# VectorE's small steps read one operand from PSUM: layer-norm variance, modulation columns and two norms' scaling in a two-block transformer kernel on one core

## What is computed

```python
# first block, layers 0 and 1
mod_x = split((silu(c) @ ada_w[layer] + ada_b[layer])[:, None, :], 6)      # and mod_c from c_ctx
h_x = modulate(rmsnorm(x, norm_g[layer, 0]), mod_x[0], mod_x[1])           # h * (1 + scale) + shift
o_x, o_c = mixer_ab(...) or mixer_c(...)                                   # attention
x = x + mod_x[2] * o_x
h_x = modulate(rmsnorm(x, norm_g[layer, 1]), mod_x[3], mod_x[4])
x = x + mod_x[5] * swiglu(h_x, ...)
# second block, 4 layers, each with three of
x = layer_norm(ALPHA * x + y, ln_g[i, j], ln_b[i, j])
# layer_norm: mu = mean(x); var = mean((x - mu)**2); (x - mu) * rsqrt(var + 1e-5) * g + b
```

## Time and profile before

| | |
|---|---|
| median of 3 runs | 2805.81 us (2800.55 to 2807.04) |
| profiled execution: span from first to last instruction | 2794.0 us |
| profiled execution: its time with what lies around the span | not listed apart; the median is 11.8 us above the span |
| TensorE matmul busy | 2636.5 us (94%) |
| GpSimd busy | 1819.7 us (65%) |
| ScalarE busy | 1467.7 us (53%) |
| VectorE busy | 1126.3 us (40%) |
| HBM | 150 GB/s |
| mean granted TensorE clock | 0.963 |

### The profile page before, as it was taken

The page is one execution under the profiler, slowest core; times in us unless marked ns, Lnnn a source line. Parts: engine busy times, 40 slices in busy tenths (PEclk is TensorE's granted clock), DMA queues, the critical chain, the costliest instruction groups (busy, mean ns, idle before and its releaser), DMA issues.

```text
span 2794.0 us, 52649 instructions
## 1 busy us (share of the span) xinstructions
PE 2636.5 (94%) x19840; PEld 2501.8 (90%) x19840; DVE 1126.3 (40%) x2642; ACT 1467.7 (53%) x2586; POOL 1819.7 (65%) x770
## 2 busy tenths in 40 slices
PE   7998889999999999989999998999999999989998
PEld 5897779999997799988899988899978999988998
DVE  5227634122155521135443365433443433553334
ACT  5336734445445554444555576555645555555655
POOL 0446647878875778863578865488645688535886
PEclk7999999999999999999999999999999999989998
DMA  6324424555553555542345543355423455323554
GB/s 228 125 102 153 146 95 166 180 178 184 183 167 126 180 168 183 179 142 81 121 151 181 185 138 128 107 189 180 157 92 121 144 181 183 127 76 121 173 180 136
DMA packets 115637, 421.75 MB, mean 151 GB/s; under 512 B 12832, under 2 KB 14112, under 8 KB 114976
## 3 DMA queue, kind: packets, MB, share of 16 engines
q1 hardware_dynamic: 115200, 417.00, 45.2%
q10 hardware_dynamic: 288, 2.62, 0.2%
HBM read 418.52 MB, written 1.05 MB: 150 GB/s over the span
## 4 chain that ended last, share of the span: by engine, by line
PE 58%; issue 18%; POOL 15%; DVE 5%; ACT 2%; DMA 1%; POOLq 0%; SPq 0%; DVEq 0%; ACTq 0%
POOL ring_low L2444 15%; PE bank L610 10%; PE bank L611 10%; PE bank L616 10%; PE bank L601 7%; PE bank L602 7%; PE bank L603 7%; PE bank L916 2%; PE bank L885 2%; PE bank L766 1%; DMA ring<-in_units 1%; PE bank L705 1%; PE bank L934 1%; PE bank L706 1%; PE bank L899 1%
## 5 line engine op out<-in xcount | busy, mean ns | idle before, releaser
L2444 POOL TENSOR_TENSOR ring_low<-ring,ring_high 128x1024 fp32r<-128x1024 f32 x766 | 1819.5, 2405 | 954.5 <-ACT ring_high L1243 744.0
L610 PE MATMUL bank<-high,ring_high 128*128 128x256 f32 (+1 forms) x3372 | 857.1, 290 | 3.2 <-ACT ring_high L1243 1.8
L611 PE MATMUL bank<-low,ring_high 128*128 128x256 f32 (+1 forms) x3372 | 849.5, 288 | 0.0
L610 PEld LDWEIGHTS bank<-high,ring_high 128*128 128x128 f32 x3372 | 647.0, 192 | 10.5 <-ACT ring_high L1243 3.5
L611 PEld LDWEIGHTS bank<-low,ring_high 128*128 128x128 f32 x3372 | 647.2, 192 | 6.5
L1475 ACT ACTIVATE ring_high<-ring 128x1024 fp32r<-128x1024 f32 x448 | 468.3, 1054 | 90.8 <-DMA ring<-in_units 90.8
L616 PE MATMUL bank<-high,ring_low 128*128 128x256 f32 (+1 forms) x3372 | 491.3, 288 | 0.3 <-POOL ring_low L2444 0.3
L616 PEld LDWEIGHTS bank<-high,ring_low 128*128 128x128 f32 x3372 | 444.9, 192 | 6.1 <-POOL ring_low L2444 0.5
L1243 ACT ACTIVATE ring_high<-ring 128x1024 fp32r<-128x1024 f32 x337 | 351.4, 1054 | 101.1 <-DMA ring<-in_units 99.7
L601 PE MATMUL bank<-hid_high,ring_high 128*128 128x256 f32 x1232 | 349.5, 284 | 9.8 <-DVE hid_low L2091 7.4
L602 PE MATMUL bank<-hid_low,ring_high 128*128 128x256 f32 x1232 | 348.6, 283 | 0.0
(11 more groups left out here) (226 smaller groups left out, 3468.3 us busy)
## 6 DMA issues: line engine op xcount, KB each, us to landing
ring<-in_units SPq DMA_DIRECT2D x785, 512.0 KB, 3.4
xt<-in_x SPq DMA_DIRECT2D x2, 1024.0 KB, 8.4
nbias<-in_bias ACTq DMA_DIRECT2D x1, 1536.0 KB, 7.2
vt<-in_mem ACTq DMA_DIRECT2D x1, 1024.0 KB, 7.1
out_x<-xt SPq DMA_DIRECT2D x8, 128.0 KB, 1.7
consts<-in_consts SPq DMA_DIRECT2D x1, 832.0 KB, 9.9
cols<-in_cols SPq DMA_DIRECT2D x1, 639.0 KB, 6.3
consts<-in_consts SPq DMA_DIRECT2D x1, 512.0 KB, 7.5
```

Of the source, the lines that this page charges most:

```text
L610: first = pe.matmul(out, w[0], x[0], start=start, stop=False)
L611: pe.matmul(out, w[0], x[1], start=False, stop=False)
L2444: pool.tensor_tensor(whole(ring_low, u), whole(ring, u), whole(ring_high, u).bitcast(fp32), ALU.subtract).then_inc(unit_ready, 1)
```

## The change

1. **Modulation columns.** ACT's copy `ada_cols_out` is gone, 24 instructions, and with it ACT's two waits and the SBUF tensor `ada_cols`. DVE waits for PE's transposes itself. Its first step becomes a `tensor_reduce` from 16 columns of the bank to 8 columns of the same bank, its second reads these from PSUM and the bias from SBUF. The bank is free for PE's next group when this second step is done.
2. In both attentions `modulations` moves from the end of DVE's step to just behind the copies of the first head's transposed probabilities, ahead of the next item's row minima.
3. **Layer norm.** L1794 and L1795 write into columns 2 and 3 of bank 6, and L1796 reads them from there.
4. **Norms f00 and f10.** The reciprocal goes to columns 0 to 255 of bank 7, and `scaled` reads it from there. Norms f01, n10 and n11 keep `rstd`.

```diff
-                def ada_cols_out(l, g, b=7):
-                    act.wait_ge(*when("ada_cols", l, g))
-                    if (l, g) != (0, 0):
-
-                        act.wait_ge(*when("mods", *((l, g - 1) if g else (l - 1, 11))))
-                    act.activation(ada_cols[:, :], banks[b][:, 0:16], ACT.Copy
-                                   ).then_inc(*mark(act_done, "ada_colsread", l, g))
...
-                def norm(st, dim, eps, b=7, between=None):
+                def norm(st, dim, eps, b=7, inverse=None):
...
-                    link(dve.reciprocal(rstd[:, 0:T], rstd[:, 0:T]))
+                    link(dve.reciprocal(rstd[:, 0:T] if inverse is None else inverse, rstd[:, 0:T]))
...
                     dve.tensor_copy(var[:, 0:4], b[:, 0:4]).then_inc(*mark(dve_done, st, "mean"))
-                    ledger.at[(st, "statsread")] = ledger.at[(st, "mean")]
                     dve.wait_ge(*when(st, "mean"))
-                    dve.tensor_scalar(var[:, 2:3], var[:, 0:1], var[:, 0:1], var[:, 2:3], ALU.mult, ALU.subtract)
-                    link(dve.tensor_scalar(var[:, 3:4], var[:, 1:2], var[:, 1:2], var[:, 3:4], ALU.mult, ALU.subtract))
-                    dve.tensor_scalar(var[:, 2:4], var[:, 2:4], 0.0, EPS_LN, ALU.min, ALU.subtract
+                    dve.tensor_scalar(b[:, 2:3], var[:, 0:1], var[:, 0:1], var[:, 2:3], ALU.mult, ALU.subtract)
+                    link(dve.tensor_scalar(b[:, 3:4], var[:, 1:2], var[:, 1:2], var[:, 3:4], ALU.mult, ALU.subtract))
+                    dve.tensor_scalar(var[:, 2:4], b[:, 2:4], 0.0, EPS_LN, ALU.min, ALU.subtract
                                       ).then_inc(*mark(dve_done, st, "var"))
+                    ledger.at[(st, "statsread")] = ledger.at[(st, "var")]
...
-                def scaled(st, l, which, s, part, at=0, tiles=range(KD)):
+                def scaled(st, l, which, s, part, rows=rstd[:, 0:T], tiles=range(KD)):
...
                             dve.scalar_tensor_tensor(out=tmp(k), in0=X(k, s), scalar=gain(l, which, s, k),
-                                                     in1=rstd[:, at:at + T], op0=ALU.mult, op1=ALU.mult
+                                                     in1=rows, op0=ALU.mult, op1=ALU.mult
...
                         out_pt(s, 0)
+                        if ada_fill(ada, 5 * s):
+                            modulations(*ada_fill(ada, 5 * s)[0])
                         if shallow:
                             lowest(s + 1, 0)
...
-                        if ada_fill(ada, 5 * s):
-                            modulations(*ada_fill(ada, 5 * s)[0])
...
-                def modulations(l, g):
+                def modulations(l, g, b=7):
 
-                    dve.wait_ge(*when("ada_colsread", l, g))
-                    parts = ada_cols[:, :].rearrange("p (m e s) -> p m e s", e=2, s=2)
-                    link(dve.tensor_tensor(sm(88, 0, 8).rearrange("p (m s) -> p m s", s=2), parts[:, :, 0, :],
-                                           parts[:, :, 1, :], ALU.add))
+                    dve.wait_ge(*when("ada_cols", l, g))
+                    link(dve.tensor_reduce(banks[b][:, 16:24].rearrange("p (m s) -> p m s", s=2),
+                                           banks[b][:, 0:16].rearrange("p (m e s) -> p m s e", e=2, s=2), AX.X, ALU.add))
...
-                    dve.tensor_tensor(dst, sm(88, 0, 8).rearrange("p (m s) -> p m s", s=2),
+                    dve.tensor_tensor(dst, banks[b][:, 16:24].rearrange("p (m s) -> p m s", s=2),
                                       bias.unsqueeze(2).to_broadcast([P, 4, 2]), ALU.add
                                       ).then_inc(*mark(dve_done, "mods", l, g))
+                    ledger.at[("ada_colsread", l, g)] = ledger.at[("mods", l, g)]
...
-                invert(0)
-                scaled("f00", 0, 1, 0, 3)
+                invert(0, banks[7][:, 0:T])
+                scaled("f00", 0, 1, 0, 3, rows=banks[7][:, 0:T])
...
-                norm("f10", D, EPS_RMS)
-                scaled("f10", 1, 1, 0, 3)
+                norm("f10", D, EPS_RMS, inverse=banks[7][:, 0:T])
+                scaled("f10", 1, 1, 0, 3, rows=banks[7][:, 0:T])
```

More of the change, by code:

```diff
@@ L188, in write_program @@
         ada_rows = sb("ada_rows", 512)
-        ada_cols = sb("ada_cols", 16)
         small = sb("small", 96)
@@ L1418, in ada_rest @@
                                 ada_rows_out(*group)
-                            else:
-                                ada_cols_out(*group)
                     for s in range(ahead):
@@ L1518, in first_rows @@
                     ada_rows_out(0, g, ADA_BANK[g])
-                def first_cols(g):
-                    ada_cols_out(0, g, ADA_BANK[g])
                 act.wait_ge(first_columns_loaded, 16)
@@ L1530, in _ @@
                 feed(6, 1)
-                first_cols(0)
                 feed(7, 1)
@@ L1537, in _ @@
                 feed(9, 1)
-                first_cols(1)
                 act.wait_ge(x_loaded[1], 16)
@@ L1545, in _ @@
                 feed(14, 1)
-                first_cols(2)
                 act.wait_ge(*when("n0", "var"))
@@ L1551, in _ @@
                 feed(17, 1)
-                first_cols(3)
                 feed(18, 1)
@@ L1777, in norm @@
                     ledger.at[(st, "statsread")] = ledger.at[(st, "var")]
-                    if between:
-                        between()
                     dve.wait_ge(*when(st, "root"))
-                    link(dve.reciprocal(rstd[:, 0:T], rstd[:, 0:T]))
+                    link(dve.reciprocal(rstd[:, 0:T] if inverse is None else inverse, rstd[:, 0:T]))
                 def centre(st, k):
@@ L1828, in norm_both, with invert @@
                     dve.wait_ge(*when(st, "root"))
-                def invert(s):
-                    link(dve.reciprocal(rstd[:, T * s:T * (s + 1)], rstd[:, T * s:T * (s + 1)]))
-                def scaled(st, l, which, s, part, at=0, tiles=range(KD)):
+                def invert(s, into=None):
+                    rows = rstd[:, T * s:T * (s + 1)]
+                    link(dve.reciprocal(rows if into is None else into, rows))
+                def scaled(st, l, which, s, part, rows=rstd[:, 0:T], tiles=range(KD)):
                     first, end = tiles[0], tiles[-1] + 1
@@ L2152, in _ @@
                 early_low(0, 8)
-                modulations(0, 0)
+                modulations(0, 0, ADA_BANK[0])
                 early_low(8, 11)
-                modulations(0, 1)
+                modulations(0, 1, ADA_BANK[1])
                 early_low(11, 13)
@@ L2161, in _ @@
                 early_low(13, 15)
-                modulations(0, 2)
+                modulations(0, 2, ADA_BANK[2])
                 gains_of(0, 0, 0, 4)
@@ L2170, in rest_of_gains @@
                     early_low(17, 18)
-                    modulations(0, 3)
+                    modulations(0, 3, ADA_BANK[3])
                     gains_of(0, 0, 4, KD)
@@ L2252, in other_stream @@
                         invert(1)
-                    scaled("f01", 0, 1, 1, 3, at=T, tiles=range(4 * n, 4 * n + 4))
+                    scaled("f01", 0, 1, 1, 3, rows=rstd[:, T:2 * T], tiles=range(4 * n, 4 * n + 4))
                 ffn("ffn_x0", aside=other_stream)
```

## The result

The changed kernel takes **2761.61 us** (median of 4 runs, 2758.45 to 2768.18) where the kernel before takes 2803.18 (4 runs, 2791.64 to 2807.04) beside it: ratio 0.9873, 95% interval 0.9848 to 0.9897, so 35.6 us (29 to 43) off. (The two medians alone differ by 41.6; with three or four runs each, the ratio is the better figure.) A later comparison gave 2761.62 us (median of 5) against 2798.69 (of 12), ratio 0.9869 (0.9846 to 0.9891), which is 36.7 us.

What follows compares the result with a forecast made beforehand. PE, busy for 94% of the span, bounds the kernel; DVE's holds by POOL count only where PE waits. 6.3 + 18.6 + 5.6 = 30.5 us off the 2794.0 span, plus 11.8 to the median, gives 2775.3 us (range 2764 to 2794).

Steps and rivals of the forecast that it cites:

- The sum, 30.5 us: Whole kernel: gain booked as 6.3 us for layer norms, 18.6 for `at0` and 5.6 for `at1`.
- The time, 2775.3 us: Whole kernel: expected span of 2763.5 us plus 11.8 us between the profiled execution's span and the median of three runs.
- Layer norms, 6.3 us: 12 layer norms: the clamp loses its hold, 8.3 us busy less 2.0; bounds 0 to 6.8 us, nothing for the clock.
- `at0`, 18.6 us: Modulation columns in `at0`, 12 groups: 11.7 us of PE waits and 6.9 us of clock; bounds 3.9 to 23.
- `ada_turn`'s 4.8: `at0`: four PE waits for ACT's rows, late through held DVE minima; 4.8 us, of which 3.2 goes.
- the first rival: Attentions: another chain, perhaps ACT, bounds them once the holds go; 12 to 16 us gained, about 2792; chance 0.22.
- `at1`, 5.6 us: Modulation columns in `at1`, 8 groups: waits for DVE copies 2.1, ACT copy 1.9, slow clock 1.7 us; bounds 1.9 to 8.
- I charge 0: Attentions: moved steps and PE's claim of bank 7, now waiting for DVE's second step, are covered and cost 0 us.
- All of that goes with the copy: `at0`: five PE waits for the ACT copy, 3.9 us, vanish because the copy is removed.
- no double rate: Norms f00 and f10: rival that a bank operand halves their tiles' time; 1.4 us off, 2774; chance 0.02.
- Their tensor operands lie in SBUF: Small DVE instructions beside POOL: what the held ones share; with an operand in PSUM they should take about 0.17 us.
- The slower rival: Moved modulation steps: POOL holds any small DVE instruction; some 25 us slower, 2831, or mild form 2806; chance 0.06, half mild.

Runs made afterwards that it cites:

- experiment 7: Kernel before with the move and PSUM operands, but ACT's copy kept, now from bank to bank, norms as before: 2775.55 us, ratio 0.9934 to the kernel before.
- experiments 1: Kernel before with the layer-norm edit alone (one-column steps write bank 6, the clamp reads it there): 2788.22 against 2797.39 us, ratio 0.9972.
- 6: Changed kernel with the first modulation step writing to SBUF and the second reading it there: 2772.97 us, ratio 0.9915 to the kernel before.
- 8: Changed kernel plus 90 small DVE instructions of twelve forms, behind tiles of the feed-forward blocks beside POOL, results unused: 2772.49 us, run once.

## Why the prediction held, and where its steps were off

**The sum, 30.5 us.** Measured: 35.6 (29 to 43) and 36.7 by the ratios, 28.4 by the stages without the luck of one execution. The sum lies between, but its two halves were off in opposite ways. The prediction has 15.7 us of waits at full clock and 8.6 us of clock, and puts the 6.3 us of the norms at the lower clock, where PE idle for 1 us counts half to the clock and half to the rest: 15.7 + 3.15 = 18.9 us of rest and 8.6 + 3.15 = 11.8 of lower clock. The timed executions show 14.4 and 21.5. So 4.5 us of the booked waits did not go or came back as others, and the lower clock gave back about 10 us more than booked. That the two nearly cancel is luck. Where the extra clock time is won isn't shown: the stages that the change touches show 13.2 of it in few profiles, and in the stretches between them it is either chance or an effect that no run isolates.

**The time, 2775.3 us,** is 13.7 us high. Of this 5.1 is the gain. The rest is the base: I carried 11.8 us from span to median, but 1.8 us lie around a span (2759.5 for 2757.7; 1.8 to 2.0 for the kernel before in its later executions), and the kernel before later had medians of 2795.6 to 2803.2 us. The three runs given were high, its profiled one ordinary. Span 2763.5 plus 1.8 would have given 2765.3.

**Layer norms, 6.3 us:** 7.6. The clamp was as said (160 ns); the distance fell to 2.83 in some norms where I had taken 3.09 from the earlier trace rows, a norm of the other kind. The upper bound of 6.8 was too tight for that reason. "PE's clock is at the lower level behind either kind of norm" holds for the kernel before (a mean of 0.50 to 0.73 between clamp and product in the eight) but less so for the change (0.63 to 0.95). So nothing booked for the clock was too little: of what the norms alone win, 8 of 9 us are lower clock (94.0 for 102.1).

**`at0`, 18.6 us:** 17.1. Waits: the values product's 4.6 went as said. `ada_turn`'s 4.8 fell to 3.0, not to 1.6: one wait of 1.75 us has nothing held ahead of it but ACT's two exponentials and a rounding (timeline of the change):

```profile
264.21 0.68 ACT L1355 ACTIVATE scr<-bank,soft 128x512 f32<-128x512 f32 x1
...
264.88 1.05 ACT L1242 ACTIVATE ring_high<-ring 128x1024 fp32r<-128x1024 f32 x1
...
265.82 0.57 ACT L1281 ACTIVATE ada_rows<-bank 4x512 f32<-4x512 f32 x1
...
266.45 0.41 PE L716 MATMUL bank<-consts,ada_rows 4*128 4x4 f32 x4 [1.75 <-ACT ada_rows L1281]
```

There the first rival was right, in one step of twelve. L933's waits, left standing, fell from 2.5 to 1.0 and made up for it; in all, PE's listed waits fell from 18.4 to 7.4 us, by 11.0 where 11.7 was booked. The clock: 10.4 us lost in the mean before, 4.6 after, so 5.8 against 6.9. "PEclk at 1.00 through both attentions" came true in the change's own profile only, the best of seven; the six others keep a stretch of some 3.4 us at the lower level in `at0`.

**`at1`, 5.6 us:** 3.7. L933 went to 0.35 us as said, the ACT copy's 1.9 us and the clock behind it went, but a claim of bank 7 waits 0.9 and `ada_turn` once 1.2. "I charge 0" for the new wait was the step that failed: it is 0.8 in `at0` and 0.9 here, 1.7 in all. (The prediction's own terms here, 2.1, 1.9 and 1.7, add up to 5.7.)

**"All of that goes with the copy"** named the wrong cause for 3.9 us: it goes with the holds. With the copy kept it was gone as well (experiment 7).

**The move at 0 us** was right only together with the operands; alone it costs 6. By the order of the programs it can't be left out either (no run tried it): the bank is now released by the second step. At the end of DVE's work this step would stand behind values that PE makes only after it has claimed the bank, and each engine would wait for the other.

**f00 and f10 at nothing, and no double rate:** 475 ns a tile, and no difference undone.

**"Their tensor operands lie in SBUF"** was too wide a rule for what is held. The profile before has counterexamples beside a running POOL instruction: 16 of the one-column steps L1794 and L1795 (264 to 274 ns, as at rest), and 6 reciprocals L1974 of 128 x 4, SBUF to SBUF (173 ns in the mean of all 44). The rule was enough for the instructions that the change touches.

**The slower rival** (the hold is not about the operand) fell by experiments 1, 6 and 8.

## What to carry to other kernels

A VectorE instruction of a few columns that takes 1 to 2 us beside a busy GpSimd is held, not working: look whether its end falls on the end of a GpSimd instruction. Give it one source in PSUM if it has two, and it costs 0.17 us; if it has one, as the clamp, either end in PSUM will do (0.16 us). Writing a two-source result to PSUM doesn't help. Then cost only the holds that TensorE feels, the clock behind those waits with them, and expect some holds to come back at the next SBUF instruction. Take what lies around the span from one execution, not from a median of others. When totals scatter, split each execution by its granted clock: in 12 executions of the kernel before, spans have a standard deviation of 4.9 us and the part without the lower clock one of 2.9.

## What was not expected of the hardware

One column was never held (154 ns, 6 times as a clamp, 5 as a copy) where three were (2127 ns); with the two one-column steps of the layer norm that is why only the clamp showed. Seven of the kernels in the table have the same program ahead of the first projection, and it took 52.0 to 60.7 us; from f10 to the first clamp, with the same program in all but three except for where f10's rows lie, PE lost 5.1 to 14.9 us to its lower clock.
